# A hybrid decoder trunk: the projection of a head's first query half moves from step 0 to step 5

## The chip, the cores and the metric

The kernel runs on one core of one Trainium2 chip. A time is the device time of one execution in microseconds (us). Engines are named as in the profile: PE is TensorE (matmuls; PEld is its weight load), DVE is VectorE, ACT is ScalarE, POOL is GpSimd, SP issues DMAs. Each engine runs its own instructions in order, and waits on semaphores for the others.

## What is computed

Two decoder layers over 1024 positions of width 1024, in float32. Only the attention branch of layer 0 matters here: 8 heads, low-rank latents, a query and key part of 64 plus a rotary part of 32.

```python
def mla(q_lat, kv_lat, k_rope, positions, ...):
    q = (rms_norm(q_lat, q_norm_g) @ w_qb).reshape(bsz, s, MLA_HEADS, QK_NOPE + QK_ROPE)
    kv = (rms_norm(kv_lat, kv_norm_g) @ w_kvb).reshape(bsz, s, MLA_HEADS, QK_NOPE + V_HEAD)
    k_nope, v = kv[..., :QK_NOPE], kv[..., QK_NOPE:]
    q_pe = apply_rope(q[..., QK_NOPE:], cos, sin)
    ...
    out = causal_attention(q_full, k_full, v)   # softmax(q k^T + causal mask) v, per head
    return out.reshape(bsz, s, MLA_HEADS * V_HEAD)
```

## The kernel before

All order is written out by hand, one program per engine, with semaphores between. The attention takes the heads in four pairs; three pairs are a hardware loop (`p`), the fourth is written behind it (`last=True`). A head is eight steps `k`, each for 128 queries, in the order of query tiles `order = [6, 7, 0, 1, 4, 5, 2, 3]`. The first head of a pair has `par` 0 ("even" below), the second `par` 1 ("odd"). The counter `i` runs over the 16 steps of a pair.

In a step TensorE does, in this order: `transpose` (the step's probabilities, L1560), `scores` for two steps ahead (L1549 to L1551, three passes of split operands), in steps 0 to 3 `project` for the next head, and `weigh` (probabilities times values, L1572). In three steps of an odd head a `turn` follows (L1587): it transposes finished output blocks of the pair, 2 blocks in steps 4 and 5, 4 blocks in step 7. So `scores` in steps 6 and 7 are those of the next head's steps 0 and 1.

`project(h, par, part)` makes a quarter of the next head's inputs. Parts 0 and 1 are the two query halves (tokens 0 to 511 and 512 to 1023; six matmuls each, L1516 to L1518), parts 2 and 3 the two key halves (one matmul call each, L1521). Every projection and every turn writes PSUM bank 0, so each has to wait until the one before has been read out:

- A query half is read by ScalarE in `nope` (scaled copy of 64 rows to `qf`, L1969) and by VectorE in `rotate` (three operations, L2398 to L2402, which also count `q_turned`). GpSimd then splits it in `head_split` (`q_hi` L477, `q_lo` L468).
- A key half is read by ScalarE alone (L1971), and split by GpSimd likewise.
- A turn is read by ScalarE (`y_hi`, L2003, into `ahi`) and then by VectorE (`y_lo`, L2432, into `alo`, which counts `y_read`).

VectorE's step `i` is: `maxima` for two steps ahead (mask added, L2412, then a reduce, L2413), `rotate` in steps 0 and 1, `outputs` (reciprocal L2418, output write L2422, which waits for `weigh`), and `y_lo` one step behind its turn. ScalarE's step is: the exponential for one step ahead (L1989), the copies of the transposed probabilities (L1996), `y_hi` one step behind its turn, `nope` in steps 0 to 3, and in step 4 the next weights.

The queries of tiles 6 and 7, which a head begins with, come from part 1; those of part 0 are first needed by the scores of its step 2, which run in step 0.

Of the kernel before, what the change touches and what calls it, by code (L numbers as in the profile page):

```python
# [122 lines left out]
def build(nc, wt, xt, pos, par, con, wqb, wkvb, wlru, wg, spill, out):  # L123
    with ExitStack() as ctx:
# [5 lines left out]
        def sem(name):  # L130
            if name not in sems:
                sems[name] = ctx.enter_context(nc.semaphore(name))
            return sems[name]
# [147 lines left out]

        turns = [(4, 6, 2), (5, 0, 2), (7, 2, 4)]

        groups_before = [sum(1 if q < 4 else 2 for q in order[:k]) for k in range(TT)]
        group_parity = [g % 2 for g in groups_before]

# [142 lines left out]
        def _(pool):  # L429
# [38 lines left out]
                nc.gpsimd.tensor_tensor(lo, src, hi.bitcast(F32), ALU.subtract).then_inc(sem("qk_lo"), 1)  # L468

            def head_split(h, part):  # L470
                if part == 0:
                    pool.wait_ge(w_used, T_L0_OUT)
                    if h >= 2:
                        pool.wait_ge(sem("scores"), TT * (h - 1))
                pool.wait_ge(sem("q_turned" if part < 2 else "k_nope"), 2 * h + part % 2 + 1)
                src, hi, _ = head_part(h, part)
                nc.gpsimd.tensor_tensor(hi, src, one_col[0:QK, :].to_broadcast([QK, HALF]), ALU.mult  # L477
                                        ).then_inc(sem("qk_hi"), 1)
                head_lo(h, part, 4 * h + part + 1)

            with pool.Fori(1, T_L0_OUT // RING) as i:
                first_tiles(i)
# [12 lines left out]
            for n, part in enumerate((2, 3, 1, 0)):  # L495
                head_lo(0, part, n + 1)
            for h in range(1, HEADS):
                for part in range(4):
                    head_split(h, part)
                if h + 1 < HEADS:  # L500
                    weight_rest(h + 1)
            for t in range(T_L0_OUT + 1, T_L0_OUT + RING):
                if t == T_L0_OUT + 2:
                    pool.wait_ge(sem("scores"), TT * HEADS)
                split(t, (t // STAGE + 1) * 16, t + 1, t - RING + 1)
# [911 lines left out]
        def _(pe):  # L1417
# [82 lines left out]
            def project(h, par, part):  # L1500
                bank = 0

                if part == 0:
                    pe.wait_ge(sem("wh_in"), h * 2)
                    pe.wait_ge(sem("wh_rest"), h)
                    pe.wait_ge(sem("dve_lat"), 6)
                if part in (0, 3):
                    pe.wait_ge(sem("k_nope"), h * 2 + part // 3)
                else:
                    pe.wait_ge(sem("q_turned"), h * 2 + part)  # L1510
                s = part % 2
                tok = halves[s]
                if part < 2:
                    for k in range(2):
                        wc = slice(k * P, (k + 1) * P)
                        nc.tensor.matmul(ps[:, bank, :], wh_hi[:, par, wc], lat_hi[:, k, tok], start=(k == 0), stop=False)  # L1516
                        nc.tensor.matmul(ps[:, bank, :], wh_hi[:, par, wc], lat_lo[:, k, tok], start=False, stop=False)
                        mm = nc.tensor.matmul(ps[:, bank, :], wh_lo[:, par, wc], lat_hi[:, k, tok], start=False,  # L1518
                                              stop=(k == 1))
                else:  # L1520
                    mm = nc.tensor.matmul(ps[0:NOPE, bank, :], wk[:, par, :], lat[:, 2, tok], start=True, stop=True)  # L1521
                mm.then_inc(sem("proj"), 1)
# [12 lines left out]
            def scores(h, par, k, step):  # L1535

                qt = order[k]
                if k in (0, 2):
                    pe.wait_ge(sem("qk_lo"), h * 4 + (3 if isinstance(step, int) and step < 2 else 4))
                if not isinstance(step, int) or step >= 2:  # L1540
                    pe.wait_ge(sem("probs"), step)
                b = 1 + 2 * (k % 2)
                n = (qt + 1) * P
                rows = slice(qt * P, (qt + 1) * P)
                hi, lo = q_hi[par][0:QK, rows], q_lo[par][0:QK, rows]
                for a in range(0, n, HALF):
                    w = min(HALF, n - a)
                    bank = ps[:, b + a // HALF, 0:w]
                    nc.tensor.matmul(bank, hi, k_hi[par][0:QK, a:a + w], start=True, stop=False)  # L1549
                    nc.tensor.matmul(bank, hi, k_lo[par][0:QK, a:a + w], start=False, stop=False)  # L1550
                    mm = nc.tensor.matmul(bank, lo, k_hi[par][0:QK, a:a + w], start=False, stop=True)  # L1551
                mm.then_inc(sem("scores"), 1)
# [24 lines left out]
            def turn(p, n, last):  # L1577

                _, first, blocks = turns[n]
                done = max(order.index(b) for b in range(first, first + blocks))  # L1580
                pe.wait_ge(sem("o_read"), (p * 16 + (8 + done + 1)) + 1)
                if n == 0:
                    pe.wait_ge(sem("k_nope"), p * 4 + (4 if last else 6))
                else:
                    pe.wait_ge(sem("y_read"), p * 3 + n + 1)
                for b in range(blocks):
                    mm = nc.tensor.transpose(ps[:, 0, b * P:(b + 1) * P], opair[:, first + b, :], ident)  # L1587
                mm.then_inc(sem("yt"), 1)

            def head_pair(p, last=False):  # L1590

                for i in range(16):
                    par, k = i // 8, i % 8
                    step = p * 16 + i
                    grp = p * 24 + (12 * par + groups_before[k])
                    transpose(k, step, grp)
                    j = i + 2
                    if not (last and j >= 16):
                        scores(p * 2 + j // 8, (j // 8) % 2, j % 8, p * 16 + j)
                    if i == 0:  # L1600
                        pe.wait_ge(sem("y_read"), p * 3 + 1)
                    if k < 4 and not (last and par == 1):
                        project(p * 2 + par + 1, 1 - par, k)
                    weigh(p * 2 + par, k, step, grp)
                    for n, (slot, _, _) in enumerate(turns):
                        if par == 1 and slot == k:
                            turn(p, n, last)
# [238 lines left out]
        def _(act):  # L1846
# [115 lines left out]
            def nope(h, part, bank=0, place_=None):  # L1962

                s = part % 2
                act.wait_ge(sem("proj"), h * 4 + ((part if place_ is None else place_) + 1))
                if place_ is None and part == 0:
                    act.wait_ge(sem("qk_lo"), h * 4)
                if part < 2:
                    nc.scalar.mul(qf[s][0:NOPE, :], ps[0:NOPE, bank, :], QK_SCALE).then_inc(sem("q_nope"), 1)  # L1969
                else:  # L1970
                    nc.scalar.copy(kf[0:NOPE, halves[s]], ps[0:NOPE, bank, :]).then_inc(sem("k_nope"), 1)  # L1971
# [34 lines left out]
            def head_pair(p, last=False):  # L2006
                for i in range(16):
                    par, k = i // 8, i % 8
                    if not (last and i == 15):
                        exps((i + 1) % 8, p * 16 + (i + 1))  # L2010
                    turned(k, p * 16 + i, p * 24 + (12 * par + groups_before[k]))
                    for n, (slot, _, _) in enumerate(turns):
                        if par == 1 and k == min(slot + 1, 7):
                            y_hi(p, n)
                    if k < 4 and not (last and par == 1):
                        nope(p * 2 + par + 1, k)
                    if k == 4 and not last:
                        head_weights(p * 2 + par + 2, par)

# [132 lines left out]
            for c in range(TT):  # L2152
                for h in range(MH):
                    n = 4 * c + h
# [38 lines left out]
        def _(dve):  # L2193
# [197 lines left out]
            def rotate(h, s, bank=0, place_=None):  # L2391

                half = slice(0, HALF)
                n = s if place_ is None else place_
                dve.wait_ge(sem("q_nope"), h * 2 + (n + 1))
                if place_ is None or n:
                    dve.wait_ge(sem("q_turned"), h * 2 + n)
# [37 lines left out]
            def head_pair(p, last=False):  # L2435
                for i in range(16):
                    par, k = i // 8, i % 8
                    if not (last and i >= 14):
                        maxima((i + 2) % 8, p * 16 + (i + 2))
                    if k < 2 and not (last and par == 1):  # L2440
                        rotate(p * 2 + par + 1, k)
                    outputs(p, par, k, p * 16 + i)
                    for n, (slot, _, _) in enumerate(turns):
                        if par == 1 and k == min(slot + 1, 7):
                            y_lo(p, n)

            for n, s in enumerate((1, 0)):
                rotate(0, s, first_banks[s], n)
# [297 lines left out]
```

## Time and profile before

| | us |
|---|---|
| median of 3 runs | 2345.33 |
| lowest and highest | 2345.32 and 2349.07 |
| the profiled execution | 2344.9 |
| its span in the trace | 2342.5 |
| PE busy in the span | 2280.9 (97%) |
| DVE, POOL, ACT busy | 1330.9, 1028.1, 903.5 |

The attention's steps lie between about 203 and 420 us of the span. A busy share of 97% is a mean over the whole kernel; the short gaps of TensorE in the attention are seen in the timeline only. A row of the timeline gives the start, the length and, in brackets, how long the engine idled before it and who released it.

### The profile page before, as it was taken

How to read it: one execution, taken by the hardware profiler on the slowest of the kernel's cores; microseconds unless marked ns; L12 is line 12 of the kernel's file. 1: busy time of each engine (PE TensorE's matmuls, PEld its weight loads, DVE VectorE, ACT ScalarE, POOL GpSimd, SP SyncE). 2: the span in 40 equal slices, each digit the busy share in tenths (PEclk: the TensorE clock that was granted, in tenths of full speed). 3: DMA queues.
4: the chain of work that ended last, by engine and by line, in shares of the span. 5: the costliest groups of instructions: out<-in, count | busy, mean ns of one | idle time of the engine just before them, and what ended most of it. 6: DMA issues, size and time to landing. Idle time of an engine off the chain costs nothing.

```text
span 2342.5 us, 31827 instructions
## 1 busy us (share of the span) xinstructions
PE 2280.9 (97%) x10415; PEld 1853.4 (79%) x10415; DVE 1330.9 (57%) x2181; ACT 903.5 (39%) x1595; POOL 1028.1 (44%) x711
## 2 busy tenths in 40 slices
PE   8998999999999999999999999999999999999997
PEld 6686777778888888888878878878788888888886
DVE  6846565258655555555671115663875555555556
ACT  4535555124433333333441114451443333333333
POOL 2413333423555555555443422224335555555554
PEclk9999999999999999999999999999999999999998
DMA  5100000311111111111231110012101111111112
GB/s 180 42 18 1 1 0 28 117 36 46 39 52 54 54 49 49 48 50 54 69 124 50 45 45 28 28 73 81 30 35 55 54 54 52 46 51 47 54 54 90
DMA packets 34583, 122.07 MB, mean 52 GB/s; under 512 B 3840, under 2 KB 3968, under 8 KB 34240
## 3 DMA queue, kind: packets, MB, share of 16 engines
q1 hardware_dynamic: 31616, 106.44, 14.6%
q10 hardware_dynamic: 2880, 14.49, 1.6%
q8 instruction: 53, 0.87, 0.2%
q14 instruction: 34, 0.28, 0.0%
HBM read 112.52 MB, written 8.39 MB: 52 GB/s over the span
## 4 chain that ended last, share of the span: by engine, by line
PE 87%; DVE 6%; ACT 3%; issue 2%; POOL 1%; DMA 1%; SPq 0%; ACTq 0%; DVEq 0%; POOLq 0%
PE ps L816 10%; PE ps L814 10%; PE ps L818 9%; PE ps L736 9%; PE ps L738 9%; PE ps L737 9%; PE ps L854 6%; PE ps L855 6%; PE ps L856 6%; PE ps L1572 2%; PE ps L1719 1%; PE ps L1723 1%; PE ps L1721 1%; PE ps L1560 1%; DMA stage<-in_wt 1%
## 5 line engine op out<-in xcount | busy, mean ns | idle before, releaser
L516 POOL TENSOR_TENSOR wlo<-stage,whi 128x512 fp32r<-128x512 f32 x308 | 397.5, 1296 | 462.3 <-ACT whi L979 457.7
L736 PE MATMUL ps<-ahi,whi 128*128 128x512 f32 x896 | 368.5, 411 | 17.3 <-DVE alo L2239 10.3
L435 POOL TENSOR_TENSOR whi<-stage,cons 128x1024 fp32r<-128x1024 f32 x64 | 127.4, 1991 | 548.6 <-PE ps L738 338.2
L738 PE MATMUL ps<-ahi,wlo 128*128 128x512 f32 x896 | 350.4, 391 | 0.0
L737 PE MATMUL ps<-alo,whi 128*128 128x512 f32 x896 | 350.0, 391 | 0.0
L979 ACT CAST whi<-stage 128x512 fp32r<-128x512 f32 x308 | 189.1, 620 | 363.6 <-POOL stage L529 180.6
L1239 DVE TENSOR_TENSOR hT<-hT,ps 128x512 f32<-128x512 f32 x352 | 238.7, 685 | 153.9 <-PE ps L856 153.9
L854 PE MATMUL ps<-hid_hi,whi 128*128 128x512 f32 x640 | 252.2, 394 | 0.7 <-POOL wlo L516 0.2
L855 PE MATMUL ps<-hid_lo,whi 128*128 128x512 f32 x640 | 249.8, 390 | 0.0
L856 PE MATMUL ps<-hid_hi,wlo 128*128 128x512 f32 x640 | 249.7, 390 | 0.0
L814 PE MATMUL ps<-ahi,whi 128*128 128x512 f32 x608 | 236.7, 389 | 0.0
L816 PE MATMUL ps<-alo,whi 128*128 128x512 f32 x608 | 236.7, 389 | 0.0
L818 PE MATMUL ps<-ahi,wlo 128*128 128x512 f32 x608 | 236.5, 389 | 0.0
L736 PEld LDWEIGHTS ps<-ahi,whi 128*128 128x128 f32 x896 | 169.1, 189 | 58.7 <-issue 19.1
L737 PEld LDWEIGHTS ps<-alo,whi 128*128 128x128 f32 x896 | 169.1, 189 | 36.4 <-issue 2.9
L738 PEld LDWEIGHTS ps<-ahi,wlo 128*128 128x128 f32 x896 | 168.8, 188 | 36.2
L816 PE MATMUL ps<-rpiece,whi 128*128 128x512 f32 x456 | 179.8, 394 | 0.0
L814 PE MATMUL ps<-rpiece,whi 128*128 128x512 f32 x456 | 179.3, 393 | 0.0
L818 PE MATMUL ps<-rpiece,wlo 128*128 128x512 f32 x456 | 178.1, 391 | 0.0
L442 POOL TENSOR_TENSOR wlo<-stage,whi 128x1024 fp32r<-128x1024 f32 x64 | 163.2, 2550 | 5.0
L854 PEld LDWEIGHTS ps<-hid_hi,whi 128*128 128x128 f32 x640 | 120.4, 188 | 31.8 <-issue 6.5
L856 PEld LDWEIGHTS ps<-hid_hi,wlo 128*128 128x128 f32 x640 | 120.6, 188 | 25.3
(324 smaller groups left out, 4096.9 us busy)
## 6 DMA issues: line engine op xcount, KB each, us to landing
stage<-in_wt SPq DMA_DIRECT2D x184, 512.0 KB, 3.6
hT<-in_xt SPq DMA_DIRECT2D x16, 256.0 KB, 6.9
hT<-in_xt ACTq DMA_DIRECT2D x8, 512.0 KB, 7.5
spill<-hT ACTq DMA_DIRECT2D x1, 4096.0 KB, 12.1
hT<-spill ACTq DMA_DIRECT2D x8, 512.0 KB, 8.6
out<-hT SPq DMA_DIRECT2D x16, 256.0 KB, 2.1
wqb_s<-in_wqb ACTq DMA_DIRECT2D x1, 1024.0 KB, 5.2
wlru_s<-in_wlru SPq DMA_DIRECT2D x1, 512.0 KB, 10.8
```

The source lines that it names most:

```text
L516: nc.gpsimd.tensor_tensor(block_lo(c), src, block_hi(c).bitcast(F32), ALU.subtract).then_inc(sem(L + "b_ready"), 1)
L736: nc.tensor.matmul(bank, hi, rhs_k[0][:, tok], start=k_first, stop=False)
L737: nc.tensor.matmul(bank, hi, rhs_k[1][:, tok], start=False, stop=False)
L738: return nc.tensor.matmul(bank, lo, rhs_k[0][:, tok], start=False, stop=k_last)
L814: nc.tensor.matmul(ps[:, bank, :], block_hi(c)[:, wk], hi, start=first and k == 0, stop=False, skip_group_check=True)
L816: nc.tensor.matmul(ps[:, bank, :], block_hi(c)[:, wk], lo, start=False, stop=False, skip_group_check=True)
L818: mm = nc.tensor.matmul(ps[:, bank, :], block_lo(c)[:, wk], hi, start=False, stop=(k == 3), skip_group_check=True)
L854: nc.tensor.matmul(bank, block_hi(b)[:, wk], hid_hi[:, j, tok], start=(j == 0), stop=False)
L855: nc.tensor.matmul(bank, block_hi(b)[:, wk], hid_lo[:, j, tok], start=False, stop=False)
L856: return nc.tensor.matmul(bank, block_lo(b)[:, wk], hid_hi[:, j, tok], start=False, stop=(j == 1))
L979: nc.scalar.copy(block_hi(c), src).then_inc(b_hi, 1)
L1239: nc.vector.tensor_tensor(h, h, ps[:, bank, :], ALU.add).then_inc(sem(L + "added"), 1)
```

## The change

Part 0 is projected in step 5 instead of step 0 (`parts_at`); parts 1, 2 and 3 stay in steps 1, 2 and 3. With it move ScalarE's `nope(…, 0)`, VectorE's `rotate(…, 0)` (in step 5 behind `outputs`) and GpSimd's `head_split(…, 0)` (behind part 3 and the next weights). Waits are renumbered for the new order. Three things are more than a move: in an odd head TensorE waits before the projection of step 5 for `y_read` of the pair's first turn; the second turn waits for `q_turned`, and VectorE reads out the first turn ahead of `outputs` in step 5 instead of behind it.

```diff
+        parts_at = {1: 1, 2: 2, 3: 3, 5: 0}
+        part_place = {1: 0, 2: 1, 3: 2, 0: 3}
...
             for h in range(1, HEADS):
-                for part in range(4):
+                for part in (1, 2, 3):
                     head_split(h, part)
                 if h + 1 < HEADS:
                     weight_rest(h + 1)
+                head_split(h, 0)
...
-                if part == 0:
+                if part == 1:
                     pe.wait_ge(sem("wh_in"), h * 2)
...
-                if part in (0, 3):
-                    pe.wait_ge(sem("k_nope"), h * 2 + part // 3)
+                if part in (1, 2):
+                    pe.wait_ge(sem("q_turned"), h * 2 + part - 1)
                 else:
-                    pe.wait_ge(sem("q_turned"), h * 2 + part)
+                    pe.wait_ge(sem("k_nope"), h * 2 + (1 if part == 3 else 2))
...
                     pe.wait_ge(sem("y_read"), p * 3 + n + 1)
+                    if n == 1 and not last:
+                        pe.wait_ge(sem("q_turned"), p * 4 + 6)
...
-                    if k < 4 and not (last and par == 1):
-                        project(p * 2 + par + 1, 1 - par, k)
+                    if k in parts_at and not (last and par == 1):
+                        if par == 1 and parts_at[k] == 0:
+                            pe.wait_ge(sem("y_read"), p * 3 + 2)
+                        project(p * 2 + par + 1, 1 - par, parts_at[k])
...
-                    if k < 4 and not (last and par == 1):
-                        nope(p * 2 + par + 1, k)
+                    if k in parts_at and not (last and par == 1):
+                        nope(p * 2 + par + 1, parts_at[k])
...
-                    if k < 2 and not (last and par == 1):
-                        rotate(p * 2 + par + 1, k)
+                    if k == 1 and not (last and par == 1):
+                        rotate(p * 2 + par + 1, 1)
+                    if par == 1 and k == 5:
+                        y_lo(p, 0)
                     outputs(p, par, k, p * 16 + i)
                     for n, (slot, _, _) in enumerate(turns):
-                        if par == 1 and k == min(slot + 1, 7):
+                        if n > 0 and par == 1 and k == min(slot + 1, 7):
                             y_lo(p, n)
+                    if k == 5 and not (last and par == 1):
+                        rotate(p * 2 + par + 1, 0)
```

Line numbers of the changed kernel are some lines higher than the profile's. On TensorE, an odd head from the scores of step 5 to the second turn. Before (L1549 to L1551 scores, L1572 weighing, L1587 turn):

```order
865 L1549 MATMUL ps<-k_hi_84,q_hi_88 128x512 [waits probs]
866 L1550 MATMUL ps<-k_lo_86,q_hi_88 128x512
867 L1551 MATMUL ps<-k_hi_84,q_lo_90 128x512
868 L1570 REGISTER_ALU [waits o_read]
869 L1572 MATMUL ps<-vtok,ptb 128x64 [waits pt_read]
...
874 L1585 REGISTER_ALU [waits o_read]
875 L1587 MATMUL ps<-cons,opair 128x128 [waits y_read]
```

The same place in the changed kernel (L1553 to L1555 scores, L1520 to L1522 projection, L1576 weighing, L1593 turn):

```order
861 L1555 MATMUL ps<-k_hi_84,q_lo_90 128x512
862 L1610 REGISTER_ALU
863 L1514 REGISTER_ALU [waits y_read]
864 L1520 MATMUL ps<-lat_hi,wh_hi 128x512 [waits k_nope]
865 L1521 MATMUL ps<-lat_lo,wh_hi 128x512
...
869 L1522 MATMUL ps<-lat_hi,wh_lo 128x512
870 L1574 REGISTER_ALU [waits o_read]
871 L1576 MATMUL ps<-vtok,ptb 128x64 [waits pt_read]
...
876 L1593 MATMUL ps<-cons,opair 128x128 [waits q_turned,y_read,o_read]
```

The six matmuls stand between scores and weighing, behind a wait for `y_read`, and the turn behind them waits for `q_turned` too.

On VectorE, step 5 of an odd head. Before (maxima, outputs, then the readout of the first turn, then the next maxima):

```order
261 L2412 TENSOR_TENSOR ps<-ps,cons 128x128 [waits probs,scores]
262 L104 REGISTER_ALU
263 L2413 TENSOR_REDUCE small<-ps 128x1 [waits dve_chain]
264 L2418 RECIPROCAL small<-small 128x1 [waits probs]
265 L104 REGISTER_ALU
266 L2422 TENSOR_SCALAR opair<-ps,small 128x64 [waits o,dve_chain]
267 L2432 ISA [waits y_hi]
268 L2432 TENSOR_TENSOR alo<-ps,ahi 128x256
```

And in the changed kernel:

```order
258 L2421 TENSOR_REDUCE small<-ps 128x1 [waits dve_chain]
259 L2440 ISA [waits y_hi]
260 L2440 TENSOR_TENSOR alo<-ps,ahi 128x256
261 L2426 RECIPROCAL small<-small 128x1 [waits probs]
262 L104 REGISTER_ALU
263 L2430 TENSOR_SCALAR opair<-ps,small 128x64 [waits o,dve_chain]
264 L2403 REGISTER_ALU
265 L2406 SCALAR_TENSOR_TENSOR rt_77<-ps,tab 32x512 [waits q_turned,q_nope]
266 L2408 SCALAR_TENSOR_TENSOR rt_78<-ps,tab 32x512
267 L104 REGISTER_ALU
268 L2410 TENSOR_TENSOR qf_79<-rt_77,rt_78 32x512 [waits dve_chain]
```

The readout of the turn (`alo`) stands directly behind the reduce, and the rotation (`rt`, `qf`) behind the output write; the next maxima follow it.

On TensorE, step 0 of an even head. Before:

```order
913 L1551 MATMUL ps<-k_hi_83,q_lo_89 128x128
914 L1516 MATMUL ps<-lat_hi,wh_hi 128x512 [waits dve_lat,wh_rest,k_nope,wh_in,y_read]
915 L1517 MATMUL ps<-lat_lo,wh_hi 128x512
916 L1518 MATMUL ps<-lat_hi,wh_lo 128x512
...
920 L1572 MATMUL ps<-vtok,ptb 128x64 [waits pt_read,o_read]
```

And in the changed kernel:

```order
912 L1553 MATMUL ps<-k_hi_83,q_hi_87 128x128 [waits probs,qk_lo]
913 L1554 MATMUL ps<-k_lo_85,q_hi_87 128x128
914 L1555 MATMUL ps<-k_hi_83,q_lo_89 128x128
915 L1576 MATMUL ps<-vtok,ptb 128x64 [waits pt_read,o_read,y_read]
916 L1576 MATMUL ps<-vtok,ptb 128x64 x3
```

The weighing follows the scores directly and takes over the wait for `y_read`.

## Rows read from the trace of the kernel before

**Rows 1.** The page, part 4: shares of the chain by engine.

```profile
PE 87%; DVE 6%; ACT 3%; issue 2%; POOL 1%; DMA 1%; SPq 0%; ACTq 0%; DVEq 0%; POOLq 0%
```

**Rows 2.** Timeline, odd head, steps 5-7: start, us, engine, line, out<-in [idle<-releaser].

```profile
303.93 1.46 PE L1572 MATMUL ps<-vtok,ptb 128*128 x12
303.95 0.39 ACT L2003 CAST ahi<-ps 128x256 f32 x1
...
304.47 0.69 DVE L2413 TENSOR_REDUCE small<-ps 128x1 f32<-128x512 f32 x1
...
305.50 0.28 DVE L2422 TENSOR_SCALAR opair<-ps,small 128x64 f32<-128x64 f32 x1 [0.28 <-PE ps L1572]
305.70 0.41 DVE L2432 TENSOR_TENSOR alo<-ps,ahi 128x256 f32 x1
...
306.17 0.44 PE L1587 MATMUL ps<-cons,opair 128*128 128x128 f32 x2 [0.78 <-DVE alo L2432]
...
311.27 1.10 PE L1572 MATMUL ps<-vtok,ptb 128*128 x8 [0.67 <-ACT ptb L1996]
...
312.90 0.86 PE L1587 MATMUL ps<-cons,opair 128*128 128x128 f32 x4 [0.53 <-DVE opair L2422]
```

**Rows 3.** Timeline, steps 0 and 1 of the same odd head.

```profile
286.53 0.44 PE L1516 MATMUL ps<-lat_hi,wh_hi 128*128 128x512 f32 x1
...
287.97 1.67 PE L1572 MATMUL ps<-vtok,ptb 128*128 x14
...
288.79 0.69 DVE L2398 SCALAR_TENSOR_TENSOR rt<-ps,tab 32x512 f32<-32x512 f32 x1 [1.43 <-ACT qf L1969]
...
290.22 0.68 DVE L2402 TENSOR_TENSOR qf<-rt,rt 32x512 f32<-32x512 f32 x1
...
290.96 0.19 PEld L1516 LDWEIGHTS ps<-lat_hi,wh_hi 128*128 128x128 f32 x1 [0.29 <-DVE qf L2402]
```

**Rows 4.** Timeline, even head, steps 6, 7, and the next head's start.

```profile
279.95 0.28 DVE L2422 TENSOR_SCALAR opair<-ps,small 128x64 f32<-128x64 f32 x1 [0.27 <-DVE small L2418]
...
281.45 0.30 DVE L2412 TENSOR_TENSOR ps<-ps,cons 128x128 f32<-128x128 f32 x1 [1.21 <-PE ps L1551]
...
282.91 1.01 ACT L1989 ACTIVATE pbuf<-ps,small 128x896 f32<-128x896 f32 x1 [2.11 <-DVE small L2413]
...
283.89 0.30 DVE L2412 TENSOR_TENSOR ps<-ps,cons 128x128 f32<-128x128 f32 x1 [0.63 <-PE ps L1551]
283.90 0.58 ACT L1996 COPY ptb<-ps 128x512 f32<-128x512 f32 x1
...
284.53 1.10 PE L1572 MATMUL ps<-vtok,ptb 128*128 x8 [0.68 <-ACT ptb L1996]
...
285.49 1.11 ACT L1989 ACTIVATE pbuf<-ps,small 128x1024 f32<-128x1024 f32 x1 [1.01 <-DVE small L2413]
```

**Rows 5.** Timeline, TensorE, step 0 of the last head.

```profile
397.28 1.75 PE L1572 MATMUL ps<-vtok,ptb 128*128 128x64 f32 x14 [0.55 <-ACT ptb L1996]
```

**Rows 6.** Timeline, step 0 of heads 0 and 2.

```profile
204.99 0.73 PE L1516 MATMUL ps<-lat_hi,wh_hi 128*128 128x512 f32 x1
...
205.48 0.95 ACT L1996 COPY ptb<-ps 128x512 f32<-128x512 f32 x2
...
260.21 0.97 ACT L1996 COPY ptb<-ps 128x512 f32<-128x512 f32 x2
...
260.49 0.73 PE L1516 MATMUL ps<-lat_hi,wh_hi 128*128 128x512 f32 x1
```

**Rows 7.** By stretch: PE, PEld, DVE, ACT, POOL busy; granted clock; DMA share.

```profile
256.00:266.00 10.00, 9.16 (x55) 8.17 (x56) 5.11 (x11) 4.72 (x11) 0.26 (x1) 0.83 0.00 0
...
414.00:424.00 10.00, 8.28 (x35) 7.06 (x36) 1.66 (x5) 1.75 (x4) 5.29 (x3) 0.66 0.51 168
```

**Rows 8.** Groups, GpSimd: names, count, busy us, mean ns, idle before.

```profile
L468 POOL TENSOR_TENSOR q_lo<-qf,q_hi 96x512 fp32r<-96x512 f32 x14 | 17.9, 1276 | 1.1
...
L477 POOL TENSOR_TENSOR q_hi<-qf,cons 96x512 fp32r<-96x512 f32 x14 | 14.5, 1037 | 119.6 <-DVE qf L2402 119.6
```

More of the change, by code:

```diff
@@ L474, in head_split @@
                         pool.wait_ge(sem("scores"), TT * (h - 1))
-                pool.wait_ge(sem("q_turned" if part < 2 else "k_nope"), 2 * h + part % 2 + 1)
+                pool.wait_ge(sem("q_turned" if part < 2 else "k_nope"), 2 * h + (2 - part if part < 2 else part - 1))
                 src, hi, _ = head_part(h, part)
@@ L478, in head_split @@
                                         ).then_inc(sem("qk_hi"), 1)
-                head_lo(h, part, 4 * h + part + 1)
+                head_lo(h, part, 4 * h + part_place[part] + 1)
             with pool.Fori(1, T_L0_OUT // RING) as i:
@@ L1501, in project @@
                 bank = 0
-                if part == 0:
+                if part == 1:
                     pe.wait_ge(sem("wh_in"), h * 2)
@@ L1538, in scores @@
                 if k in (0, 2):
-                    pe.wait_ge(sem("qk_lo"), h * 4 + (3 if isinstance(step, int) and step < 2 else 4))
+                    pe.wait_ge(sem("qk_lo"), h * 4 + (3 if k == 0 else 4))
                 if not isinstance(step, int) or step >= 2:
@@ L1964, in nope @@
                 s = part % 2
-                act.wait_ge(sem("proj"), h * 4 + ((part if place_ is None else place_) + 1))
-                if place_ is None and part == 0:
-                    act.wait_ge(sem("qk_lo"), h * 4)
+                act.wait_ge(sem("proj"), h * 4 + ((part_place[part] if place_ is None else place_) + 1))
+                if place_ is None and part < 2:
+                    act.wait_ge(sem("qk_lo"), h * 4 - part)
                 if part < 2:
@@ L2393, in rotate @@
                 half = slice(0, HALF)
-                n = s if place_ is None else place_
+                n = 1 - s if place_ is None else place_
                 dve.wait_ge(sem("q_nope"), h * 2 + (n + 1))
```

## The prediction

> **What bounds the kernel now.** I read the chain of waits on the page first: 87% of the span hangs on TensorE, 6% on VectorE, 3% on ScalarE [rows 1]. The change touches only the attention, which runs from about 203 to 420 us, so I then read the timeline there, all engines together. TensorE goes through eight steps for each of eight heads (transposes, next scores, in some steps a projection, then the weighing), and it is busy except for short gaps. An odd head waits 0.78 us before the second turn (L1587) [rows 2], an even head 0.68 us in its last step, before the weighing (L1572), for ScalarE's copy [rows 4]. So a microsecond counts where TensorE idles; what the other engines gain or lose counts only if it reaches one of those gaps. Steps are numbered from 0, "even" heads are the first of a pair (par 0), "odd" the second.
>
> **Work removed and added: none.** The same six matmuls, one ScalarE scaling, three VectorE operations and two GpSimd splits of a query half run elsewhere. In step 0 of a head they cost TensorE 287.97 - 286.53 = 1.44 us [rows 3]; in step 5 they cost the same 1.44. So I sum only idle time of TensorE: what appears, what vanishes.
>
> **Term 1, odd heads, first wait in step 5.** All projections and turns share PSUM bank 0. In an odd head the first turn has just been written there, so the moved projection waits until it is read out: ScalarE's ahi copy, which is early (303.95 + 0.39), then VectorE's alo subtraction (L2432), which the change puts behind the maxima of step 7. Those end at 304.47 + 0.69 = 305.16 [rows 2]. With the subtraction's 0.41 and some 0.03 to the next instruction the projection starts at 305.60. TensorE would have been free at 303.93, where the weighing starts now. Idle: +1.67 us.
>
> **Term 2, odd heads, second wait in step 5.** The second turn also writes bank 0, and now waits for the rotation of the projection. VectorE does it behind `outputs`, which waits for the weighing. Before, the turn starts at 306.17 after 0.78 idle, so the weighing ended at 305.39; VectorE's output write started at 305.50 and let the next instruction start at 305.70, 0.31 behind that end [rows 2]. The rotation takes 290.22 + 0.68 - 288.79 = 2.11 us, and TensorE goes on 0.06 us behind it [rows 3]. ScalarE's scaling (0.6 us) is hidden by the 1.46 us weighing. Idle 0.31 + 2.11 + 0.06 = 2.48 in place of 0.78: +1.70 us. Terms 1 and 2 fall in the odd heads of three pairs; the last head projects nothing. 3 x (1.67 + 1.70) = **+10.1 us**.
>
> **Term 3, even heads, steps 5 to 7.** There the projection in step 5 waits for nothing, since bank 0 holds no turn. But the rotation lies on VectorE in front of the maxima that the last step hangs on. On the clock of before: outputs at 279.95, free 0.28 later at 280.23, rotation to 282.34, so the maxima that started at 281.45 start at 282.33, 0.87 us late against TensorE's own shift [rows 4]. They release the exponential (282.91), that the copy (283.90), that the weighing (284.53), each directly: the gap of 0.68 becomes 1.55. 4 x 0.87 = **+3.5 us**. GpSimd is no part of it: its two operations, 1.04 and 1.28 us, sit on an engine that idled 119.6 us over 14 times in front of the first of them [rows 8]. They end at 282.34 + 2.32 = 284.66, and the scores that need them run just ahead of 286.53 [rows 3]; 1.5 us or more of room, and the shift of the odd head's start widens it.
>
> **Term 4, the next step 0.** Its exponential moves by less (VectorE's next maxima, at 283.89, are pushed to about 284.15): 285.49 becomes 285.75, its end 286.86, the first copy 0.58 more, the weighing 287.50 with the release. TensorE, 0.87 late and without the projection, is ready at 286.53 + 0.87 = 287.40. So **+0.1** for each of three heads. The last head, which has no projection before either, idles 0.55 there [rows 5]; that is eaten by the delay: -0.5. Together -0.2.
>
> **Term 5, step 1.** The second half's projection waited 0.29 us for the first half's rotation to leave bank 0 [rows 3]; seven times. **-2.0 us.**
>
> **Term 6, step 0 of even heads.** The projection covered the wait for the probability copy. At pairs 2 to 4 TensorE is free at 260.49 and the first copy done at 260.21 + 0.58 = 260.79: +0.36 each with the release. At the first head it is free at 204.99, the copy done at 206.06: +1.1 [rows 6]. All of that lies in stretches of the lower clock (granted clock 0.50 of full, the 1.2 GHz level; below), where idle time displaces work worth half as much: (3 x 0.36 + 1.1) / 2 = **+1.1 us**.
>
> **Sum:** 10.1 + 3.5 - 0.2 - 2.0 + 1.1 = **+12.5 us**. The profiled execution took 2344.9 us for a span of 2342.5, 0.4 below the median of 2345.3, so I add to the median: 2357.8, say **2358**. Bounds of the terms: term 1 at least 1.3 (the subtraction starts as soon as the reduce drains) and at most 2.0; term 2 between 1.3 and 2.2, since the turn's wait is a register instruction; term 3 between 0.5 and 1.1; together (three, three and four times) about -4 and +3.
>
> **The clock.** TensorE's granted clock falls to the 1.2 GHz level at the start of pairs 2, 3 and 4, each time after the odd head's closing gaps (0.78, 0.67 and 0.53 us of idle within 8 us) [rows 2]. The mean of 0.83 over 10 us means 3.4 us at half speed, worth 1.7 us; the last such fall, after the gappier last head, has 0.66 over 10 us, or 6.8 us [rows 7]. With 1.67 + 2.48 us of idle close together in step 5 of an odd head, the fall should come earlier, on steps 6 and 7, where ScalarE's chain leaves gaps that a slower TensorE fills. I take the bill as unchanged: one fall per pair.
> The Trainium skill, "TensorE: Matmul & The Clock Gate", "Terms", prices a throttled stretch at its length times the share of pulses left out; the trace agrees, 3.4 us at half being worth 1.7. The same page, "A second HAM failure mode: psum-queue depth-cycling", says that a TensorE which idles briefly but often between groups of matmuls swings between the levels and pays for each return. That speaks against this change, and is rival B.
>
> **Rivals.**
> A, forecast: the two waits in odd heads, clock bill unchanged, 2358. Chance 0.60.
> B, the clock adds: another low stretch in each pair (the odd head's step 5 and the old place both), 3 x 1.7 = +5, 2363; or stretches of 6.8 us, or falls in even heads too after the 1.55 us gap, up to +12, 2370. For it: the falls of before need only 2 us of idle. Against it: the even heads' 0.68 us and the last head's 0.55 us brought no fall, and one fall spends the idle that would cause the next. Chance 0.22.
> C, the clock gives back: with step 0 free of waits the falls vanish, -5: 2353. For it: little; idle grows. Chance 0.12.
> D, not slower: both waits of step 5 lie in the shadow of waits that are there already. The place is VectorE's queue in odd heads. It decides if the alo subtraction ends before TensorE reaches the projection (303.93) and the rotation before the weighing ends; then terms 1 and 2 are gone and 2.4 remain, 2348, or with C's clock 2343, faster. Against: the subtraction stands behind maxima that need the scores TensorE has just made, and the rotation stands behind an operation that waits for that weighing, so neither can be early. Chance 0.06.
> That the change does nothing is excluded by the order of instructions.
>
> **How the numbers follow.** A measurement of this kernel tells 0.2%, 4.7 us, from no change. A, B and C all lie above 2350. D is split, two thirds within, one third faster: faster 0.02, same 0.04, slower 0.94. The range takes A with its bounds (2354 to 2361), C and most of B: 2351 to 2368. It leaves out D and B's far end, some 0.12.
>
> **What would show it.** In odd heads but the last: an idle of 1.5 to 2 us before the first matmul of the projection, released by VectorE's alo, and one near 2.5 us before the second turn, released by VectorE's qf. In even heads: 1.5 us before the last weighing. In step 1: no idle. The attention ends near 432 us in place of 420; everything behind it keeps its length. Wrong would be: idle in step 5 under 2 us in all, or six and more low-clock stretches in place of four.

## The result, and the profile after

| | us |
|---|---|
| changed kernel, median of 6 runs | 2381.34 (2370.51 to 2385.10) |
| kernel before, median of 6 runs | 2345.45 (2344.47 to 2349.07) |
| ratio | 1.0142, interval 1.0124 to 1.0160 |
| profiled execution of the changed kernel, its span | 2379.25, 2377.4 |

The change makes the kernel 36 us slower by the medians (the ratio, 1.0142, amounts to 33 us: four of the six runs lie at 2379 to 2385, two at 2371). The forecast was 2358 and the range ended at 2368: the direction was right, the size was not.

Each wait that the forecast named is there. The timeline of the changed kernel, all engines, step 5 of the first odd head (lines are 4 to 8 higher than before; L1520 to L1522 is the projection, L1576 the weighing, L1593 the turn):

```profile
251.34 0.40 PE L1555 MATMUL ps<-k_hi,q_lo 96*128 96x512 f32 x1
...
252.10 0.69 DVE L2421 TENSOR_REDUCE small<-ps 128x1 f32<-128x512 f32 x1
252.71 0.41 DVE L2440 TENSOR_TENSOR alo<-ps,ahi 128x256 f32 x1
...
253.25 0.49 PE L1520 MATMUL ps<-lat_hi,wh_hi 128*128 128x512 f32 x1 [1.52 <-DVE alo L2440]
...
254.74 1.45 PE L1576 MATMUL ps<-vtok,ptb 128*128 x12
...
256.30 0.28 DVE L2430 TENSOR_SCALAR opair<-ps,small 128x64 f32<-128x64 f32 x1 [3.11 <-PE ps L1576]
256.62 0.69 DVE L2406 SCALAR_TENSOR_TENSOR rt<-ps,tab 32x512 f32<-32x512 f32 x1
...
258.05 0.68 DVE L2410 TENSOR_TENSOR qf<-rt,rt 32x512 f32<-32x512 f32 x1
...
258.88 0.41 PE L1593 MATMUL ps<-cons,opair 128*128 128x128 f32 x2 [2.69 <-DVE qf L2410]
```

That is the step of [rows 2], one pair earlier. The projection waits 1.52 us for the first turn's readout, the turn waits 2.69 us for the rotation, where it waited 0.78. The last weighing of the even heads, 0.68 in [rows 4], waits 1.64. TensorE's own view of the waits over the attention says how often:

```profile
PE ps L1576 <- ACT ptb L2004: 15.6, 20, 1.7
PE ps L1593 <- DVE qf L2410: 8.1, 3, 2.7
PE ps L1520 <- DVE alo L2440: 4.6, 3, 1.5
```

Now the whole attention, from its first scores to the next stage's first matmul, before and after. The columns are the stretch, its length, the busy time of PE, PEld, DVE, ACT and POOL, the granted clock of TensorE, and DMA:

```profile
197.60:419.70 222.10, 205.19 (x1296) 170.79 (x1297) 124.45 (x310) 113.11 (x276) 80.90 (x68) 0.95 0.03 10
```

```profile
201.50:454.00 252.50, 219.92 (x1295) 186.26 (x1296) 123.99 (x310) 114.38 (x276) 79.21 (x68) 0.89 0.03 8
```

The attention is 30.4 us longer. TensorE idles 32.6 us of it instead of 16.9, which is 15.7 more, near what was forecast. The same matmuls also take 14.7 us more. Added up over 1 us slices, TensorE is at the 1.2 GHz level for 24 us of the attention before, and for 58 us after: 34 us more at half speed, which fits the 14.7 us. The stretches of 3.4 us in [rows 7] have become these, in two of three pairs:

```profile
328.00:346.00 18.00, 17.07 (x72) 15.89 (x71) 6.24 (x16) 6.23 (x14) 1.26 (x1) 0.53 0.00 0
392.00:410.00 18.00, 17.07 (x75) 15.95 (x74) 5.61 (x14) 6.44 (x14) 1.99 (x2) 0.53 0.00 0
```

A mean of 0.53 over 18 us is 17 us at half speed. Each begins about 1 us after the second turn of an odd head has started, behind its wait of 2.7 us, and goes on into the next pair although TensorE is busy 17 of those 18 us. In the first pair it is 7 us there and 3.4 more in the next step 0. One of the four even heads has a stretch too, 10 us, right behind its wait of 1.64 us (which ends at 297.06):

```profile
297.00:308.00 11.00, 10.94 (x49) 10.55 (x50) 2.27 (x9) 3.91 (x9) 0.00 (x0) 0.53 0.00 0
```

(Another 3.9 us of the difference between the two traces lies ahead of the attention, where the programs are alike: low-clock time there differs from one execution to the next.)

### The profile page after: what moved, and what is told of

It reads as the page before. It is cut to its first block, busy times and chain, and to the rows that moved or that the text cites. A ratio compares the mean times of both kernels' runs of the same rounds, so it can differ in the third digit from the quotient of the medians.

```text
span 2377.4 us, 31840 instructions
## 1 busy us (share of the span) xinstructions
PE 2300.0 (97%) x10415; PEld 1872.0 (79%) x10415; DVE 1329.8 (56%) x2181; ACT 904.7 (38%) x1595; POOL 1028.3 (43%) x711
## 4 chain that ended last, share of the span: by engine, by line
PE 86%; DVE 6%; ACT 3%; issue 2%; POOL 1%; DMA 1%; ACTq 0%; SPq 0%; DVEq 0%; POOLq 0%
PE ps L820 9%; PE ps L818 9%; PE ps L822 9%; PE ps L740 9%; PE ps L742 9%; PE ps L741 9%; PE ps L858 6%; PE ps L860 5%; PE ps L859 5%; PE ps L1576 2%; PE ps L1727 1%; PE ps L1731 1%; PE ps L1729 1%; PE ps L1564 1%; PE ps L614 1%
## 5 line engine op out<-in xcount | busy, mean ns | idle before, releaser
L740 PE MATMUL ps<-ahi,whi 128*128 128x512 f32 x896 | 370.0, 413 | 16.4 <-DVE alo L2247 10.1
```

What stands on the lines that cost most here:

```text
L740: nc.tensor.matmul(bank, hi, rhs_k[0][:, tok], start=k_first, stop=False)
```

## Experiments

**The theory.** The change costs its idle time, and on top half of the low-clock time that follows this idleness. **The rivals.** The excess comes from one kind of head only; or it is something else than the clock (the waits themselves, VectorE's longer queue, GpSimd's later splits).

### One kind of head at a time

The switch is per head: a head whose `par` is in `MOVED` projects part 0 in step 5, the other keeps it in step 0, and the waits follow.

```diff
-        parts_at = {1: 1, 2: 2, 3: 3, 5: 0}
+        def parts_at(par):
+            return {1: 1, 2: 2, 3: 3, 5: 0} if par in MOVED else {0: 0, 1: 1, 2: 2, 3: 3}
```

> Only the projections that run in even heads move to step 5; those of odd heads stay in step 0, so no turn shares step 5 with a projection and the two long waits of odd heads (1.52 and 2.69 us in the changed kernel) are gone. Idle time by my terms: even heads' last gap 3.5 us, uncovered copy 1.1, step 1 -1.2, last head -0.5, together +3. Theory (the excess over my sum is TensorE's clock, and it comes from the odd heads' waits): 2348 to 2351, three low-clock stretches at the pair starts as before. Rival (the even heads' gap of 1.64 us brings down the clock by itself): a low stretch behind the 1.64 us gap in some pairs, 2353 to 2360. Rival (the excess has nothing to do with which head): half of the excess, 2363.

> Only the projections that run in odd heads move to step 5. Idle time: waits in step 5 3 x 3.4 = 10.1 us, uncovered copy in step 0 of odd heads 3 x 0.7, step 1 -0.9, together +11. Theory (odd heads' waits bring the clock down for long): 2367 to 2377, low-clock stretches of 7 us and more from step 5 of odd heads on. Rival (idle alone): 2357. Rival (it takes the even heads' gap too): 2357 to 2362.

Even heads alone: 2360.53 (2352.88 to 2368.49), ratio 1.0080, interval 1.0054 to 1.0105. Odd heads alone: 2366.12 (2363.49 to 2367.10), 1.0092, 1.0075 to 1.0109. Against 2344.12 for the kernel before these are +16 and +22, together 38, about the whole change. My theory that the excess hangs on the odd heads alone fell: it gave the even heads 2351 at most. The rival on the even heads' gap came within 0.5 us of its range (2360), and odd heads alone stayed 1 us under the theory's range. In the trace of even heads alone, low stretches of 3.4 us stand behind the 1.64 us gap of heads 0 and 2:

```profile
228.00:238.00 10.00, 8.84 (x53) 8.03 (x54) 5.09 (x13) 5.30 (x12) 1.19 (x2) 0.83 0.00 0
286.00:296.00 10.00, 8.27 (x51) 7.61 (x51) 5.09 (x13) 5.78 (x12) 1.17 (x2) 0.83 0.00 0
```

But this trace is of the fastest of the five runs (2352.88), and it shows no added low clock: 21 us of the attention against 24 before. The falls have moved; the 9 us that this run lost are idle time (26 us against 17). The clock's part shows only in the runs without a trace: at 2364 and 2368 us their mean granted clock is 0.982 and 0.980, here 0.989.

The trace of odd heads alone has 43 us of low clock: 13.7 us behind the 2.69 us wait in the first two pairs, 20 us in the last head, and nothing behind the same wait in the third pair (it ends at 378.73):

```profile
253.00:268.00 15.00, 13.98 (x54) 12.49 (x55) 5.60 (x13) 4.88 (x10) 2.31 (x2) 0.55 0.00 1
378.00:393.00 15.00, 12.43 (x84) 10.85 (x85) 8.60 (x20) 6.89 (x15) 3.04 (x3) 1.00 0.00 0
```

The trace of even heads alone also showed a term that I had made too small. This is TensorE in step 0 of heads 2 and 4, where the projection used to cover the copy; it waits 1.2 us at full clock:

```profile
262.25 1.77 PE L1603 MATMUL ps<-vtok,ptb 128*128 x14 [1.20 <-ACT ptb L2037]
...
320.95 1.88 PE L1603 MATMUL ps<-vtok,ptb 128*128 x14 [1.22 <-ACT ptb L2037]
```

### Matmuls in the waits

Matmuls on operands of the projection, with a result that nobody reads, go in front of a wait, into a bank that no one uses in that step. Nothing else changes; the kernel does more work, and none in place of other work.

```diff
+            def filler(par, bank, n):
+
+                for _ in range(n):
+                    nc.tensor.matmul(ps[:, bank, :], wh_hi[:, 1 - par, 0:P], lat_hi[:, 0, 0:HALF], start=True, stop=True)
...
                         if par == 1 and k == 5:
+                            filler(par, 4, FILL.get("project", 0))
                             pe.wait_ge(sem("y_read"), p * 3 + 2)
```

> The changed kernel with matmuls whose result nobody reads in front of the two waits of step 5 in odd heads: 6 before the projection (1.4 us), 11 before the second turn (2.5 us), into a bank that is free there. The waits end when they ended; TensorE is busy meanwhile. Theory (clock): the long low stretches of odd heads go, 2358 to 2363, what is left being stretches behind the even heads' gap. Rival (the excess is waiting time or something else in the change): 2379 to 2385, or more for the added work.

Measured: 2384.48 (2380.33 to 2391.09), ratio 1.0177, interval 1.0153 to 1.0201. By its number the theory failed: this is the rival's range. The trace says why: the odd heads' stretches did go (first row, steps 5 to 7 of the first odd head and on into the next), but low clock stood behind the even heads' gap instead, which was left open (second row), and in the first head and the last pair. In all 73 us of the attention were low.

```profile
250.00:272.00 22.00, 20.18 (x122) 16.02 (x121) 10.54 (x25) 9.40 (x25) 8.07 (x8) 1.00 0.00 1
298.00:312.00 14.00, 12.75 (x65) 12.33 (x66) 4.23 (x12) 6.14 (x14) 0.59 (x1) 0.63 0.00 0
```

So filling some of the waits is no test of the clock. Filling all of them is:

> The changed kernel with unread matmuls in front of every gap of the attention: 6 and 11 at the two waits of odd heads, 6 at the even heads' 1.64 us gap, 5 in step 0 where the projection was, 1 to 4 at the small ones. Filling the odd heads' waits alone left 2384, with low clock behind the even heads' gap and in step 0. Theory (all of the excess over the idle sum is low clock that follows idle): low-clock time in the attention from 58 us to under 25, and 2357 to 2364. Rival (something else in the change keeps the clock low): 2380 or more.

Measured: 2358.76 (2357.54 to 2359.19), ratio 1.0062, interval 1.0045 to 1.0079. The attention has no low clock but 3.4 us at its very start:

```profile
201.10:435.30 234.20, 226.97 (x1426) 186.06 (x1427) 123.84 (x310) 113.55 (x276) 79.78 (x68) 0.99 0.03 9
```

131 matmuls more make the changed kernel 22.6 us faster (20.5 by the means of the runs). The two long waits still end when they ended: the projection starts 1.91 us after the last scores of its step in both kernels, the turn 4.13 us after the weighing here and 4.14 without fillers. Only TensorE's idleness is gone:

```profile
252.85 0.49 PE L1543 MATMUL ps<-lat_hi,wh_hi 128*128 128x512 f32 x1 [0.16 <-DVE alo L2474]
...
258.47 0.41 PE L1621 MATMUL ps<-cons,opair 128*128 128x128 f32 x2
```

The added matmuls can only take time of their own, and the waits did not become shorter, so the 22.6 us are clock.

> The kernel before, with 1 to 4 matmuls whose result nobody reads in front of each of TensorE's gaps in steps 0, 3, 4, 5, 6 and 7, of about the length of the gap. The work computed is the same. Theory (idle between matmuls brings the clock down, at the pair starts too): the falls at pairs 2 to 4 and in the last head go, 14 us at half speed, so 2337 to 2343. Rival (falls do not follow from these gaps): 2345 to 2350, since the added matmuls delay a little.

The same on the kernel before gave 2341.88 (2339.22 to 2346.01), ratio 0.9991, interval 0.9982 to 1.0001. It was run again to narrow that:

> The filled kernel of before once more, with more rounds: 2339 to 2343, 1 to 4 us below the kernel before, all of it low-clock time at pairs 2 to 4 and in the last head.

2341.40 (2339.89 to 2346.72), ratio 0.9987, interval 0.9978 to 0.9995: 3 us faster than the kernel before, the only version here that is. Its attention takes 216.8 us (the row is from the first of the two runs of this kernel):

```profile
201.50:418.30 216.80, 210.00 (x1348) 171.22 (x1349) 124.21 (x310) 113.16 (x276) 80.05 (x68) 0.99 0.03 10
```

With the clock up on both sides the move costs 2358.76 - 2341.88 = 16.9 us (234.2 - 216.8 = 17.4 in the attention). This is its price in idle time. The rest of the 36 us, 22.6 less the 2.8 to 3.7 that the kernel before loses to its own falls, is clock: about 19 by the medians, 18 by the means.

### A wait without the move

In the kernel before, the second turn of odd heads (three times) waits for three VectorE operations of no use. In the profile its wait becomes 2.8 us; no projection moves.

```diff
+                        pe.wait_ge(sem("stall"), p + 1)
...
+                    if par == 1 and k == 5 and not last:
+                        for dst, rows in ((rt1, a32), (rt2, a32), (rt1, b32)):
+                            ins = nc.vector.tensor_tensor(dst[rows, 0:HALF], tab[rows, 0:HALF], tab[rows, HALF:S], ALU.add)
+                        ins.then_inc(sem("stall"), 1)
```

> The kernel before, no projection moved, with one wait more: in step 5 of odd heads (three times) the second turn waits for three operations on VectorE that compute nothing of use, which makes its wait of 0.78 us some 2.1 us longer. Idle +6.3 us. Theory (idle costs its length and half of the low-clock time that follows): 2355 to 2362, with stretches longer than 3.4 us around the pair starts. Rival (a wait costs its length): 2350 to 2352.

Measured: 2365.04 (2364.34 to 2365.66), ratio 1.0088, interval 1.0071 to 1.0105. Three waits, 6.1 us longer in sum, cost 20 us. Even the theory had expected less (2362 at most). With each wait of 2.8 us come 17 us of low clock, which set in 1.3 us before the wait ends:

```profile
254.54 0.69 PE L1589 MATMUL ps<-cons,opair 128*128 128x128 f32 x2 [2.81 <-DVE rt L2450]
```

```profile
253.00:271.00 18.00, 15.94 (x61) 14.33 (x62) 6.73 (x15) 5.24 (x11) 0.00 (x0) 0.53 0.00 0
314.00:332.00 18.00, 15.48 (x57) 13.89 (x58) 7.18 (x15) 4.87 (x10) 0.00 (x0) 0.53 0.00 0
376.00:394.00 18.00, 16.05 (x63) 14.47 (x63) 6.61 (x15) 5.42 (x12) 0.00 (x0) 0.53 0.00 1
```

> The stalled kernel e8 with 12 unread matmuls (2.8 us) in front of the stalled turn; the turn runs when it ran in e8. Theory (the 14 us that e8 paid beyond its 6.1 us wait are low clock from TensorE's idleness): the three stretches of 17.1 us go, 2348 to 2352. Rival (the delay of VectorE or the wait itself slows the rest): 2365 as e8.

Measured: 2350.36 (2349.90 to 2352.55), ratio 1.0027, interval 1.0016 to 1.0039. The same wait, filled (L1566 is the filler, L1624 the turn):

```profile
250.84 2.98 PE L1566 MATMUL ps<-lat_hi,wh_hi 128*128 128x512 f32 x12
253.84 0.44 PE L1624 MATMUL ps<-cons,opair 128*128 128x128 f32 x2
```

```profile
253.00:271.00 18.00, 16.06 (x108) 13.65 (x107) 10.20 (x23) 7.93 (x18) 2.30 (x2) 1.00 0.00 1
```

The three stretches are gone (one of 3.4 us stays at a pair start, as in the kernel before) and 14.7 us with them; 5.2 us are left, about the length added to the waits. The delay of VectorE and of the turn is the same in both, so the rival that blames them is out.

> As the stalled kernel before (e8), but with one VectorE operation behind the second turn's wait in place of three: the wait of 0.78 us in odd heads becomes some 1.45 us, three times, idle +2.1 us. If the low-clock time grows with the idle time, 2349 to 2354 with stretches between 3.4 and 17.1 us; if it goes by a step between 1.5 and 2.8 us of wait, 2346 to 2348 with the three old stretches of 3.4 us.

Measured: 2353.21 (2351.40 to 2355.86), ratio 1.0037, interval 1.0025 to 1.0049. The waits of 1.50 us (idle +2.1) cost 8.1 us, more than the step between 1.5 and 2.8 us allowed (2348 at most). In the trace one of the three stretches grew to 13.7 us, two stayed at 3.4.

### Shortening the waits

> The changed kernel with the second turn moved from step 5 to step 6 of odd heads, so that the rotation lies behind TensorE's work of step 6. The wait of 2.69 us goes, the third turn waits some 0.6 us more. Idle by my terms: 12.5 - 3 x 1.7 - 3 x 0.8 + 3 x 0.6 = +7. Theory: 2352 without any added low clock, up to 2368 with stretches from the 1.52 us wait and the closing gaps; more than 5 us better than my term for the wait alone (2381 - 3 x 2.5 = 2373.8), since the clock falls less. Rival (waits only): 2373 to 2376.

The second turn in step 6 (`turns = [(4, 6, 2), (6, 0, 2), (7, 2, 4)]`): 2369.14 (2363.88 to 2378.68), ratio 1.0120, interval 1.0089 to 1.0150. 12 us less than the changed kernel for 3 x 2.2 us less in front of the second turn: it now waits 0.51 us for the rotation, the projection 1.52 as ever (in all, TensorE idles 4.4 us less in the attention, 28.1 us). The median lies between the theory (2368 at most) and the 2373 to 2376 of the waits alone, and the runs spread over both, so this one settles little.

> The changed kernel with VectorE's order altered in step 5: in odd heads the readout of the first turn stands ahead of the maxima, and in all heads the rotation ahead of the output write. By the trace the first wait falls from 1.52 to some 0.9 us, the second from 2.69 to some 1.4, the even heads' gap from 1.64 to some 0.8: idle 3 x 1.9 + 4 x 0.8 = 9 us less. Theory (idle time and the low-clock time that follows it both count): 2355 to 2368, more than 9 us below the changed kernel. Rival (waits alone): 2372.

```diff
+                    if early and DVE_EARLY:
+                        y_lo(p, 0)
                     if not (last and i >= 14):
                         maxima((i + 2) % 8, p * 16 + (i + 2))
...
+                    if full and moved and k == 5 and DVE_EARLY:
+                        rotate(p * 2 + par + 1, 0)
...
                     outputs(p, par, k, p * 16 + i)
```

Measured: 2355.84 (2354.91 to 2366.72), ratio 1.0049, interval 1.0032 to 1.0067. Waits of 1.01 and 1.64 us in odd heads, 0.58 for the 1.64 us gap in even ones: these are 9 us less, as expected. But step 0 of the odd heads, which had no gap, now waits 1.1 us, so TensorE idles only 2.3 us less in the attention than in the changed kernel (30.3 us; the trace is of the slowest of the five runs, 2366.72). The time is 25 us less. Low clock falls from 58 to 30 us in this trace, 20 of them in the last head; the four faster runs have a higher mean granted clock still, 0.989 to 0.992 against 0.985.

> The moved projection at its best: VectorE's readout and rotation early (e5), and unread matmuls in the gaps that are left. Idle against the filled kernel of before: waits of 1.0 and 1.64 us for 0.78 in odd heads (+1.9 each), 0.6 in step 6 of even heads, 1.1 in step 0 of most heads. By that 2341.9 + 5.6 + 2 + 7 - 3 - 2 = 2350 to 2354. If it were under 2342, the move itself would be worth having.

Measured: 2354.87 (2352.89 to 2356.89), ratio 1.0046, interval 1.0034 to 1.0058, 0.9 us above what was expected. With no low clock in the attention at all, the best form of the move is still 13 us behind the filled kernel of before. Moving this projection is not worth having in any form tried.

## Why the prediction was wrong, point by point

- **Terms 1 and 2** (odd heads, +10.1): 1.52 and 2.69 us for 1.67 and 2.48 forecast; (1.52 + 2.69 - 0.78) x 3 = 10.3. Right in place, cause and size. The readout of a turn behind the maxima, and the rotation behind the output write, were read from the order of instructions.
- **Term 3** (even heads, +3.5): 1.64 for 0.68, four times, 3.8. Right.
- **Term 4** (-0.2): 0.15 us of idle in the odd heads' step 0 where it shows, for 0.1 forecast, and the last head's 0.55 us became 0.21. Right.
- **Term 5** (-2.0): too large. The wait in front of the projection of step 1 is gone, but the one in front of the projection of step 2 has grown (0.22 us where it was 0.14). By the weight loads, on which I read the 0.29 us, that is about -1.5; TensorE's matmuls themselves idled only 0.08 us there before.

```profile
311.16 0.19 PEld L1525 LDWEIGHTS ps<-lat,wk 128*64 128x64 f32 x2 [0.23 <-DVE qf L2410]
```

- **Term 6** (step 0 of even heads, +1.1): mis-sized. I took 0.36 us from a pair start of before, where the clock was low and TensorE slow, and halved it. With the clock up (even heads alone) it is 0.83, 1.20, 1.22 and 1.39 us, together 4.6. With that the sum is 16.0 instead of 12.5, and 16.5 with term 5 put right, against 16.9 measured between the two filled kernels. A gap measured under a low clock is not the gap under a high one.
- **"I take the bill as unchanged: one fall per pair."** This is the step that failed. Forecast, as before, 24 us of low clock in the attention, measured 58. It is worth about 19 of the 36 us, of which the forecast had none. The number of stretches hardly grew: the prediction counted four before and would have been warned by six, and by the same count there are five in the attention and one that starts as it ends. Their length did, and no sign was set on that.
- **Rival B** had the mechanism, and the price of it far too small. It let a stretch last 6.8 us at most; with 2.7 us of idleness it lasted 17. Its rule in the Trainium skill ("TensorE: Matmul & The Clock Gate", "A second HAM failure mode: psum-queue depth-cycling") is that short and frequent idling makes TensorE swing between the levels. The traces agree: none of the waits here exceeds 2.9 us, and three that grew by 6.1 us in all cost 20. Its "against" (the even heads' 0.68 us brought no fall) was read correctly, but says little of a gap of 1.64 us, which brought one in one of four heads.
- **The range.** Taking 6.8 us as the bound on stretches not yet seen was what cut it at 2368. It was not even the longest seen: the trace of before has 10 us of low clock where the attention begins, the stretch on which term 6 rests for head 0. It starts at 197.2, 1.4 us behind the end of a wait of 2.41 us. (In the changed kernel's trace the same wait is followed by 3.4 us only.)

```profile
195.78 1.13 PE L1497 MATMUL ps<-wkvb_s,lat 128*128 128x512 f32 x2 [2.41 <-ACT vtok L1960]
```

```profile
197.00:208.00 11.00, 10.25 (x33) 8.34 (x34) 4.56 (x7) 5.22 (x9) 0.00 (x0) 0.53 0.00 0
```

- **Rival D** (not slower) and rival C (clock gives back): neither; the wait for `y_read` and the one for `q_turned` decide as written.

What stays open: why one wait brings a fall and its equal in the next pair does not, and why a stretch lasts 3.4 us at one place and 17 or 24 us at another with TensorE nearly as busy. Executions of one kernel differ in it too: the changed kernel's six runs have mean granted clocks from 0.975 (2385.10 us) to 0.985 (2370.51 us), while the filled one's four stay within 1.7 us.

## What to carry to other kernels

On a kernel that TensorE bounds, an idle microsecond is not priced at a microsecond: here it cost two to four, since the clock often fell with it and stayed low for 3 to 24 us. Count the added idle time of TensorE, then ask what the granted clock does behind each gap, and give that its own wide range; the longest low stretch of the trace before is no bound. Unread matmuls in the gaps are both the test (they separate waits from clock) and, where a free PSUM bank is at hand, a small gain; and before work is moved out of a step, look at what it covers there, at the clock that will then hold.

## What the runs showed of the hardware that was not expected

- 2.8 us of idleness, three times, brought 3 x 17 us at the 1.2 GHz level, with TensorE busy 16 of each 18 us. The stretches seen in the attention in all runs last from 3.4 to 24 us.
- A wait does not bring a fall each time. Of the nine unfilled waits of 2.7 to 2.8 us (changed kernel, odd heads alone, stalled kernel) eight did; of the sixteen gaps of 1.6 to 1.7 us before the last weighing of even heads (changed kernel, even heads alone, two waits filled, turn later) seven did; of the three waits of 1.64 us in front of the second turn (vector early) none did.
- "Busy" in the profile did not always keep the clock up. Ahead of the attention 32 matmuls of one column each (L626) fill 4.6 us without a gap, and in nine of the fourteen traces the clock falls inside them or within 1.2 us behind them. In the other five, that of the kernel before among them, it does not fall there. From the filled kernel of before:

```profile
168.58 4.57 PE L626 MATMUL ps<-cons,sqb 128*128 128x1 f32 x32
```

```profile
168.00:173.00 5.00, 5.00 (x36) 4.88 (x35) 0.87 (x2) 0.27 (x1) 0.00 (x0) 0.80 0.00 0
173.00:178.00 5.00, 5.00 (x13) 3.94 (x14) 0.87 (x2) 0.70 (x3) 1.01 (x1) 0.51 0.00 0
```

- A kernel can be made faster by giving TensorE more to do: 131 matmuls that nobody reads took 22.6 us off the changed kernel, 53 took 3 us off the one before.
